# Decode attention of a hybrid decoder step: cached values issued by GpSimd, cached keys by SyncE

## The reference, cut to what matters

```python
# layer 0, for each of the DEC_BATCH = 8 sequences
ka_all = concatenate([cache_win_k_a[j], ka])       # (1024 + 8) positions, 8 heads x 64
va_all = concatenate([cache_win_v_a[j], va])
o_a = dilated_attn_sample(qa, ka_all, va_all, win_s)
k_past = cache_k_b[j, page_table]                  # 8 pages of 128 positions, 4 heads x 128
v_past = cache_v_b[j, page_table]
o_b = diff_attn_sample(qb, k_past, v_past, kb, vb, lam)
hs = hs + ab_merge(o_a, o_b, subln_g[j], lam_init, w_out[j])
```

## Time and profile before

| what | us |
|---|---|
| median of 3 runs | 2634.75 |
| lowest and highest run | 2629.86, 2636.74 |
| the profiled execution, its own time | 2627.97 |
| its span, first to last instruction | 2626.2 |
| TensorE busy in the span | 2484.7 (95%) |
| VectorE busy | 1061.6 (40%) |
| ScalarE busy | 675.2 (26%) |
| GpSimd busy | 196.7 (7%) |
| DMA traffic of SyncE's queue (q1) | 179.60 MB |
| DMA traffic of GpSimd's queue (q0) | 47.64 MB |

### The profile page before, as it was taken

How to read it: one execution, slowest core, us unless ns; L and a number is a source line. 1 busy time by engine, 2 the same in 40 slices (tenths; PEclk the granted TensorE clock), 3 DMA queues, 4 the chain that set the end, 5 groups by cost and what they waited for, 6 DMA issues and landing times.

```text
span 2626.2 us, 40065 instructions
## 1 busy us (share of the span) xinstructions
PE 2484.7 (95%) x16305; PEld 2296.1 (87%) x16305; DVE 1061.6 (40%) x2204; ACT 675.2 (26%) x1180; POOL 196.7 (7%) x239
## 2 busy tenths in 40 slices
PE   7999988888889989999999999999899999999997
PEld 6778866555569989999999999889899999999996
DVE  4312066555774713333332333456233333333324
ACT  5221134355663311111111011154111111111112
POOL 0020100144331000000000000030000000000000
PEclk9999999999999999999999999998999999999998
DMA  4331299925552101111111111111110111111101
GB/s 160 108 102 51 110 352 406 360 92 176 176 168 68 33 33 49 50 49 49 49 33 33 49 46 36 34 45 33 49 49 32 48 48 48 48 48 49 49 9 68
DMA packets 119678, 229.27 MB, mean 87 GB/s; under 512 B 6259, under 2 KB 82372, under 8 KB 116971
## 3 DMA queue, kind: packets, MB, share of 16 engines
q1 hardware_dynamic: 113731, 179.60, 20.0%
q0 software_dynamic: 5808, 47.64, 5.2%
HBM read 209.32 MB, written 51.41 MB: 99 GB/s over the span
## 4 chain that ended last, share of the span: by engine, by line
PE 86%; issue 4%; DVE 4%; DMA 2%; ACT 2%; SPq 2%; POOL 0%; DVEq 0%; ACTq 0%
PE ps L1783 72%; PE ps L769 2%; PE ps L1817 2%; PE ps L804 2%; PE ps L785 2%; DMA kraw<-cache_win_k_a 2%; SPq L892 1%; PE ps L1872 1%; PE ps L2090 1%; PE ps L1911 1%; DVE ws L614 1%; DVE pT L568 0%; SPq L895 0%; POOL sm L1053 0%; DMA xin<-x_prompt 0%
## 5 line engine op out<-in xcount | busy, mean ns | idle before, releaser
L1783 PE MATMUL ps<-xn,ws 128*128 128x384 f32 (+1 forms) x6744 | 1121.7, 327 | 20.1 <-DVE ws L614 15.9
L1783 PEld LDWEIGHTS ps<-xn,ws 128*128 128x128 f32 x6744 | 1114.8, 188 | 22.7 <-issue 21.9
L1783 PE MATMUL ps<-hh,ws 128*128 128x384 f32 (+1 forms) x3168 | 536.9, 330 | 8.7 <-issue 8.7
L1783 PEld LDWEIGHTS ps<-hh,ws 128*128 128x128 f32 x3168 | 530.9, 190 | 9.2 <-issue 9.2
L1618 DVE TENSOR_TENSOR act_h<-act_s,ps 128x384 f32<-128x384 f32 x132 | 70.2, 532 | 871.5 <-ACT act_s L1236 871.5
L1236 ACT ACTIVATE act_s<-ps 128x384 f32<-128x384 f32 x132 | 62.5, 473 | 1230.4 <-PE ps L1783 1119.6
L1605 DVE TENSOR_TENSOR x<-ps,x 128x384 f32<-128x384 f32 (+1 forms) x552 | 284.9, 532 | 209.1 <-PE ps L1783 207.3
L1783 PE MATMUL ps<-wp,xn 128*128 128x512 f32 (+1 forms) x1080 | 245.4, 389 | 0.0
L1783 PEld LDWEIGHTS ps<-wp,xn 128*128 128x128 f32 (+1 forms) x1080 | 196.3, 182 | 48.9
L614 DVE TENSOR_TENSOR ws<-wraw,ws 128x2048 fp32r<-128x2048 f32 x69 | 157.3, 2282 | 9.1 <-ACT ws L609 9.1
L609 ACT ACTIVATE ws<-wraw 128x2048 fp32r<-128x2048 f32 x69 | 129.5, 1904 | 46.7 <-PE ps L1783 44.8
(11 more groups left out here) (209 smaller groups left out, 1773.4 us busy)
## 6 DMA issues: line engine op xcount, KB each, us to landing
wraw<-w_gate SPq DMA_DIRECT2D x22, 1024.0 KB, 5.4
wraw<-w_up SPq DMA_DIRECT2D x22, 1024.0 KB, 5.4
wraw<-w_down SPq DMA_DIRECT2D x22, 1024.0 KB, 4.8
kraw<-cache_win_k_a SPq DMA_DIRECT2D x8, 2048.0 KB, 14.8
vraw<-cache_win_v_a SPq DMA_DIRECT2D x8, 2048.0 KB, 11.9
kraw<-cache_k_b SPq DMA_DIRECT2D x64, 256.0 KB, 6.2
vraw<-cache_v_b SPq DMA_DIRECT2D x64, 256.0 KB, 11.1
o_wk_s<-cache_win_k_a POOLq DMA_DIRECT2D x8, 2032.0 KB, 8.6
```

The source lines that it names most:

```text
L1783: r = mm(out, w(a), m(b_), start=(i == 0 and q_ == 0), stop=(i == n - 1 and q_ == 2))
```

## The change

The loads of cached values leave SyncE's stream and go to GpSimd's. SyncE keeps the keys: its loop now has two waits and two kinds of load, both for `b + 1`, with the page numbers read at the top. GpSimd issues the first value window after it has stored the last 128 rows of the last projection group (before: at 45 projection groups), reads the first 8 page numbers, then loads the tables as before, stores the samples' rows, issues the first value pages, and runs a loop of its own over sequences 1 to 7. Both engines read the page table. No computing instruction changes.

```diff
--- before.py
+++ after.py
@@ -897,38 +897,20 @@
             sp.dma_start(ptab[:], d["page_table"].rearrange("b n -> (b n)").rearrange("(a n) -> a n", a=1)).then_inc(page_table_loaded, 16)
             sp.wait_ge(proj_done, 45)
             load_window(0, kraw, "cache_win_k_a", dec_k_loaded)
-            load_window(0, vraw, "cache_win_v_a", dec_v_loaded)
             sp.wait_ge(page_table_loaded, 16)
             pages = page_numbers(0)
             sp.wait_ge(proj_done, 54)
             load_pages(pages, kraw, "cache_k_b", dec_k_loaded)
-            load_pages(pages, vraw, "cache_v_b", dec_v_loaded)
-            turned, used = (sp.alloc_register(n) for n in ("turned", "used"))
-            sp.reg_mov(turned, 8)
-            sp.reg_mov(used, 0)
-            sp.wait_ge(dec_k_turned, 8)
-            load_window(1, kraw, "cache_win_k_a", dec_k_loaded)
-            with sp.Fori(0, DB - 2) as b:
+            turned = sp.alloc_register("turned")
+            sp.reg_mov(turned, 0)
+            with sp.Fori(0, DB - 1) as b:
                 pages = page_numbers(b + 1)
                 sp.reg_add(turned, turned, 8)
                 sp.wait_ge(dec_k_turned, sp.snap(turned))
-                load_pages(pages, kraw, "cache_k_b", dec_k_loaded)
-                sp.reg_add(used, used, 1)
-                sp.wait_ge(dec_values_done, sp.snap(used))
-                load_window(b + 1, vraw, "cache_win_v_a", dec_v_loaded)
+                load_window(b + 1, kraw, "cache_win_k_a", dec_k_loaded)
                 sp.reg_add(turned, turned, 8)
                 sp.wait_ge(dec_k_turned, sp.snap(turned))
-                load_window(b + 2, kraw, "cache_win_k_a", dec_k_loaded)
-                sp.reg_add(used, used, 1)
-                sp.wait_ge(dec_values_done, sp.snap(used))
-                load_pages(pages, vraw, "cache_v_b", dec_v_loaded)
-            pages = page_numbers(DB - 1)
-            sp.wait_ge(dec_k_turned, 16 * (DB - 1))
-            load_pages(pages, kraw, "cache_k_b", dec_k_loaded)
-            sp.wait_ge(dec_values_done, 2 * DB - 3)
-            load_window(DB - 1, vraw, "cache_win_v_a", dec_v_loaded)
-            sp.wait_ge(dec_values_done, 2 * DB - 2)
-            load_pages(pages, vraw, "cache_v_b", dec_v_loaded)
+                load_pages(pages, kraw, "cache_k_b", dec_k_loaded)
 
 
             sp.wait_ge(sample_rows_stored, 16 * (2 + 2 * DB))
@@ -1016,6 +998,11 @@
                            .rearrange("t h n -> t (h n)"))
                     pool.dma_start(dst, tok[:, t % 3]).then_inc(rows_stored[t % 3], 16)
                 if g == 5:
+                    pool.wait_ge(page_table_loaded, 16)
+                    window = d["cache_win_v_a"][0, 0:1].rearrange("a (p j) h n -> (a p) j (h n)", j=8)
+                    pool.dma_start(vraw[0][:], window).then_inc(dec_v_loaded[0], 16)
+                    first_pages = [d["cache_v_b"][0, bass.ds(pool.value_load(ptab[0:1, j:j + 1], min_val=0, max_val=NPHYS - 1), 1)]
+                                   .rearrange("a p h n -> p (a h n)") for j in range(NPAGE)]
                     pool.wait_ge(proj_done, 54)
                     for name, dst in (("decA", dmask[:, 0, 0:PAST]), ("newA", dnew[:, 0]), ("newB", dnew[:, 1]),
                                       ("comb0", comb[:, 0]), ("comb1", comb[:, 1])):
@@ -1032,6 +1019,28 @@
                     dst = d["o_wk_s" if g == 1 else "o_wv_s"][0].rearrange("b t h n -> b t (h n)")
                     for b in range(DB):
                         pool.dma_start(dst[b, PAST - T:PAST], toks[b * T:(b + 1) * T, g]).then_inc(sample_rows_stored, 16)
+
+
+            def value_rows(b):
+
+                pages = [pool.value_load(ptab[0:1, bass.ds(b * NPAGE + j, 1)], min_val=0, max_val=NPHYS - 1) for j in range(NPAGE)]
+                window = d["cache_win_v_a"][0, bass.ds(b, 1)].rearrange("a (p j) h n -> (a p) j (h n)", j=8)
+                return window, [d["cache_v_b"][0, bass.ds(page, 1)].rearrange("a p h n -> p (a h n)") for page in pages]
+
+            pages = first_pages
+            for j, src in enumerate(pages):
+                pool.dma_start(vraw[1][:, j], src).then_inc(dec_v_loaded[1], 16)
+            used = pool.alloc_register("used")
+            pool.reg_mov(used, 0)
+            with pool.Fori(1, DB) as b:
+                window, pages = value_rows(b)
+                pool.reg_add(used, used, 1)
+                pool.wait_ge(dec_values_done, pool.snap(used))
+                pool.dma_start(vraw[0][:], window).then_inc(dec_v_loaded[0], 16)
+                pool.reg_add(used, used, 1)
+                pool.wait_ge(dec_values_done, pool.snap(used))
+                for j, src in enumerate(pages):
+                    pool.dma_start(vraw[1][:, j], src).then_inc(dec_v_loaded[1], 16)
 
             pool.wait_ge(sample_rows_stored, 16 * (2 + 2 * DB))
```

## The result

The changed kernel takes 2642.97 us (median of 8 runs, 2636.04 to 2650.13) against 2634.39 (8 runs, 2629.86 to 2636.74): ratio 1.0035, 95% interval 1.0022 to 1.0048. It is **slower by 0.35%, some 9 us**. Its profiled execution took 2640.96 us, with a span of 2639.3.

A forecast was written before the change was run, and what follows sets the result against it. Decode was taken as bound by the DMA engines. Bytes and order, including dip and first window, gave +3.3 us, 4 KB value-page packets -1.6: together +1.7, from 2634.75 to 2636.4 us, range 2625 to 2650.

The forecast's parts named there:

- rival A: Value loads in decode: GpSimd's queue moves bytes more slowly, 348 GB/s against 407; +15.5 us, 2650; chance 0.16.
- B: Rival, decode: GpSimd can't issue value loads in time; +77 us at three times its issue work, about 2712; chance 0.09.
- C: Rival, decode: two queues keep the DMA engines fuller, all at 432 GB/s with keys first; -9.8 us, 2625; chance 0.18.
- Bound by bytes, 10.41 us a step: Decode from 382.59 to 486.72 us: DMA engines bound it, ten steps of 10.41 us each, TensorE 1.16 us a step behind.
- my signs: Listed marks in the new profile, among them value loads landing within 8 us and key pages taking longer than 6.
- The dip: Decode at 370 to 380 us, 265 GB/s: third sequence's key pages asked for about 5 us sooner, worth 3.5 us.
- Who goes first, one load landed ahead: Decode's two queues: 16 KB value packets go before 2 KB key pages, one load of 2.1 MB landed early; sum +3.3 us.
- The first window's share: First value window, issued by GpSimd after the store at 327.64: some 0.6 MB fall behind 335 us, 1.5 us.
- As long as bytes bound the stage, both wash out: Decode's start: first key pages up to 4 us later beside first value pages, second key window earlier; taken as nothing.
- The end: End of decode: key pages and TensorE's two last steps still end last, as before; no change taken.
- 4 KB packets worth -1.6: Value pages in decode: GpSimd's 4 KB packets instead of 2 KB gain 1.6 us, bounds none to -4.9.
- Issue work on GpSimd: Decode: 9 value DMAs at 0.54 us plus 5.8 us of page numbers, 10.6 of 20.8 us a sequence; cost taken as nothing.

The follow-up runs named there:

- g1: The kernel before with one queue and page numbers read early, but every load from the second sequence on issued by GpSimd; ratio to before 0.9981, decode 166.4 us.
- e4: The kernel before, all loads by SyncE in the same order, loop written out, next sequence's page numbers read behind the value window; ratio 0.9986, decode 166.6 us.
- e1: The changed kernel with its first value window back on SyncE at 45 projection groups; ratio to before 1.0027, decode 176.9 us.
- f1: e1 plus GpSimd holding the first value pages until the first key pages have landed; ratio to before 1.0017, decode 173.7 us.
- e2: The changed kernel with the first value pages held until the first key pages have landed; ratio to before 1.0011, decode 179.3 us.
- h1: e4 with the second key window issued ahead of the first value pages; ratio to before 0.9980, decode 166.5 us.
- e5: The changed kernel with roles swapped: from the second sequence on GpSimd loads keys, SyncE values; ratio to before 1.0020, decode 172.7 us.
- h4: Another split than the changed kernel's: SyncE loads all windows, GpSimd all pages from the second sequence on; ratio to before 1.0097, decode 192.8 us.
- e3: The changed kernel with each value window issued only after its sequence's key pages have landed; ratio to before 1.0032, decode 179.1 us.
- h2: e2 with every later value load issued one key transpose later; ratio to before 1.0043, decode 177.4 us.

## Why the prediction was right, and where it was not

The time fell into the range (2625 to 2650), and the sign of my sum was right, but its size was not: +1.7 us forecast as no change, and 1.0035 measured, beyond the bound of 0.3% that I had set and so in the outcome to which I gave 0.25. That the range holds it is in part luck: its upper half stood there for rival A, which did not happen. No rival did: A and B (GpSimd's queue slow) are excluded by g1, and C by the splits, of which none is faster.

Step by step:

*Bound by bytes, 10.41 us a step:* right on average. The pace of the steady stretch is 10.3 with two queues, but no step is like the mean: they take 9.3 to 12.6 us. Of my signs one more failed: value windows should have landed within 8 us and took 11.6 (median), about as long as the key windows' 12.0.

*The dip:* right in place and cause. The key pages of the third sequence are issued 0.2 us after their buffer is free (375.16, against 370.88 + 4.10), where it was 5.9 us before, and the dip is filled. The price is about two thirds of the 3.5 us worked out: e4, which moves the page-number reads and writes the loop out, wins 2.3 us up to the last key transposes. That its whole decode is 3.6 us shorter fits my 3.5 by luck, since 1.3 of it are the last value product at a higher clock.

*Who goes first, one load landed ahead:* right. 59.4 MB before and 62.1 after were the forecast; over the slightly longer stretch 59.9 and 62.5 were measured. At 390 GB/s 2.6 MB is 6.6 us. The first window's share of it is 31.04 - 30.18 = 0.86 MB (GpSimd's traffic, changed against e1) for my 0.6. That this window's time costs a measurable amount is not shown: e1's interval overlaps that of the changed kernel.

*"As long as bytes bound the stage, both wash out":* **this is the step that failed**, a cost taken as nothing while its cover went. I had the first key pages up to 4 us late. They came 5.5 us late in decode's time (15.2 against 9.7 us in), TensorE fell behind, its buffers stayed full, and the DMA engines ran out of work: 188 GB/s at 355 to 360. The first 35 us moved at 364 GB/s instead of 399, 1.2 MB or 3.0 us. Bytes bound the stage only while something is asked for. f1 and e2 take this one competition away, and the ratio falls from e1's 1.0027 to 1.0017 and from 1.0035 to 1.0011; only the second step is clear of noise, and just.

*The end:* not foreseen. I had the last wait stay. In the changed kernel everything but the last value pages is in before the last key transposes, and the DMA engines go idle (120 GB/s at 495 to 500). From 475.06 on TensorE waits for no load, so what its clock costs there is not hidden: those transposes take 6.54 us, 2.4 more than the 4.10 of a free set.

*The account:* the 14th step ends 8.5 us later in decode's time (160.7 for 152.2). 2.6 MB more at 389 GB/s are 6.6 us, where I had 2.7 MB; the rest is the rate, 59.9 MB at 389 instead of 394, 1.9 us. That in turn is the start (+3.0), the end (490 to 496.3 at 351 and 120 GB/s instead of 407, +1.6) and the dip, 10 us x (381 - 265) / 407 = -2.9, together +1.7. Behind the 14th step TensorE is 2.5 us quicker (15.5 for 18.0): 1.3 since the last key pages are there, and 1.3 since the last value product takes 1.95 us for 3.25. I had taken nothing for it. So decode is 6.0 longer for my +1.7: the bytes as worked out, the dip nearly so, the start and the end left out, and 1.6 us of gain that didn't come.

*TensorE's clock:* not in the prediction at all. Told from TensorE's side, the 6.0 us are 8.9 of slower work less 2.9 of shorter idling. It is so in every split kernel: TensorE is busy for 153 to 159 us of decode at a granted clock of 0.91 to 0.97, against 149 to 150 at 0.99 to 1.00 in the kernel before, e4, g1 and h1. This doesn't make the clock the cause of the loss. While bytes bound the stage, a slower set of transposes can be made up by a shorter wait, as the pace of 10.30 us a step shows. It counts where no load is waited for behind it, as from 475.06 on. No run held the clock apart from the waits, so its share is open.

*4 KB packets worth -1.6:* wrong. g1's pages moved at 374 GB/s in 4 KB packets, SyncE's at 378 in 2 KB. The row width decides here and not the packet, or something else that both share; that wasn't tried.

*Issue work on GpSimd:* right. Its page issues in the loop took 0.55 us each on average (54 of them 29.6 us), and the page numbers about 5.7 (from 376.59 to 382.30):

```profile
376.04 0.55 POOL L1043 DMA_DIRECT2D vraw<-cache_v_b  x1 [0.34 <-issue]
382.30 0.55 POOL L1039 DMA_DIRECT2D vraw<-cache_win_v_a  x1 [5.71 <-issue]
```

The Trainium skill's rule that VectorE's copies hold up GpSimd's descriptors (its page SBUF — State Buffer, section "SBUF: two separate sides") cost nothing that shows: the issues are as long as the 0.54 us of the earlier trace rows, and g1, with all loads through GpSimd, kept 406 GB/s beside the same copies.

**What is shown and what is open.** Shown: a split in two queues loses in each of the three ways of dividing the loads that were tried (changed, e5, h4), with the start held only just (e2), one queue in order of need with the page numbers read ahead wins with either engine, and two queues take turns by packets. Nearly shown: part of the changed kernel's loss is made at the start. Holding the first value pages wins 5 of its 8.6 us by e2, whose interval just misses the changed kernel's, and 3 by f1, whose interval overlaps e1's. Not settled: what exactly makes the rest, and how much of it is the lower clock. My theory of values landing too early predicted that e3 and h2 would recover it, and both failed; they moved the waits from keys to values. Why the waits gather in every fourth step was not found out.

## What to carry to other kernels

In this stage, bound by the DMA engines, a second queue added no bandwidth (405 GB/s for 407) and took away the order: the queues alternate packet by packet, so at each turn a load with 16 KB packets moves eight times the bytes of an urgent one with 2 KB packets (measured for 16 against 4 KB: 0.75 to 0.15 MB). First look for what keeps the one queue from being fed, here 5.8 us of page-number reads between two issues, and move that: e4, g1 and h1 won 0.14 to 0.2% where the split lost 0.35%. A cost that "washes out" in a stage bound by bytes does so only if requests are still outstanding while the engine is late.

## What the runs showed of the hardware

TensorE's granted clock reacts to the gathered waits. After the waits of up to 1.7 us before the change the 32 key transposes take 3.9 to 4.1 us. After the changed kernel's four waits they take 5.2 to 6.5, at a granted clock of 0.72 and 0.55 in two of them, so partly at the level of 1.2 GHz, while an unhindered set runs at 2.4 GHz throughout (1.00). These are the changed kernel's stretches over three sets of key transposes, and g1's over its one set behind a wait of 2.18 us:

```profile
392.70:397.90 5.20, 5.20 (x35) 5.05 (x35) 2.08 (x3) 2.19 (x4) 2.19 (x4) 0.72 0.97 395
475.10:481.60 6.50, 6.50 (x35) 6.50 (x35) 2.08 (x3) 2.20 (x4) 3.64 (x7) 0.55 0.98 395
496.30:500.30 4.00, 3.97 (x35) 3.58 (x35) 2.08 (x3) 3.01 (x7) 3.14 (x6) 1.00 0.43 151
```

```profile
465.40:470.70 5.30, 5.30 (x34) 5.25 (x35) 2.07 (x3) 2.20 (x4) 2.41 (x5) 0.68 1.02 433
```

So many small waits were cheaper for TensorE than the same time in a few long ones, which cost 1.1 to 2.4 us on top of each. The wait as listed doesn't decide alone: 1.72 us in e1 was followed by a set of 5.41 us, 1.80 in e4 by one of 3.88. How much of it reaches the end of decode wasn't measured apart, except that the 2.4 us behind the wait at 475.06 meet no later wait for a load.

One copy of VectorE from SBUF to SBUF ended with GpSimd's memset. In the changed kernel the first of these copies in decode took 1.36 us instead of 0.40, and GpSimd's memset ran beside it:

```profile
338.16 1.36 DVE L1481 COPY qcur<-qblk 128x128 f32<-128x128 f32 x1
338.47 0.97 POOL L1010 MEMSET dmask<- 128x1024 f32 x1
```

The copy ends at 339.52, the memset at 339.44. In e2 (337.52 and 337.44), in e1 (338.83 and 338.74) and before (336.29 and 336.21) the copy likewise ends 0.08 to 0.09 us behind the memset, so it looks as if the one held the other; no run tried it. In the changed kernel and e2 TensorE's second set of transposes then started after 2.03 and 2.04 us of idling, for 1.47 before, and the granted clock was 0.50 from 341 to 345 in both. The first key pages were waited for until 350.80 anyway, so this copy alone cost decode nothing that shows.
